# Rotary key projection of a diffusion backbone on one Trainium2 core: two products a chunk in place of three

## The reference

```python
D_MODEL, Q_LORA, KV_LORA, QK_ROPE, LRU_WIDTH, DEPTH = 1024, 384, 256, 32, 1024, 2
h = rms_norm(x, g_pre_mix) * (1.0 + sc1) + sh1
proj = h @ w_in            # columns: 384 query latent | 256 key/value latent | 32 rotary key | 1024 lru_x | 1024 lru_gate | 2048 merge
# query latent, kv latent: RMS norm, then up-projections to heads, attention
# rotary key (32 columns): axial rotation for the sample, shared by all 8 heads
# lru_x: centred convolution, two gates, a forward and a backward scan (RG-LRU)
# lru_gate: gelu;  merge: sigmoid gates of the two branches
```

## Time and profile before

| | |
|---|---|
| Median of 3 runs | 1290.33 us (1288.76 to 1290.85) |
| Profiled execution, device time | 1289.83 us |
| Its span, first to last instruction | 1288.0 us |
| PE busy | 1259.7 us (98%), 7748 matmuls |
| PEld busy | 1163.7 us (90%) |
| DVE busy | 803.5 us (62%), 1424 instructions |
| ACT busy | 660.5 us (51%), 1170 instructions |
| POOL busy | 18.4 us (1%) |
| DMA | 199.39 MB, mean 155 GB/s |
| Mean granted TensorE clock | 0.998 |
| Chain that ended last | PE 87%, DVE 5%, ACT 4%, issue 2%, DMA 2% |

### The profile page before, as it was taken

The page is one execution under the profiler, slowest core; times in us unless marked ns, Lnnn a source line. Parts: engine busy times, 40 slices in busy tenths (PEclk is TensorE's granted clock), DMA queues, the critical chain, the costliest instruction groups (busy, mean ns, idle before and its releaser), DMA issues.

```text
span 1288.0 us, 20162 instructions
## 1 busy us (share of the span) xinstructions
PE 1259.7 (98%) x7748; PEld 1163.7 (90%) x7748; DVE 803.5 (62%) x1424; ACT 660.5 (51%) x1170; POOL 18.4 (1%) x41
## 2 busy tenths in 40 slices
PE   6999999999999999999999999999999999999998
PEld 4999999978889999998889999998798899999886
DVE  2697584764858877743368786756566884433423
ACT  5379873754464333342266989457445533333422
POOL 0000000200000000000000000011000000000000
PEclk9999999999999999999999999999999999999999
DMA  9645555333346766545425546463225464444451
GB/s 335 202 121 175 191 153 195 105 115 120 119 128 205 228 212 212 164 139 176 123 63 166 156 132 203 130 227 112 102 77 162 149 200 131 132 131 131 156 164 49
DMA packets 138275, 199.39 MB, mean 155 GB/s; under 512 B 10330, under 2 KB 70980, under 8 KB 138180
## 3 DMA queue, kind: packets, MB, share of 16 engines
q1 hardware_dynamic: 138180, 198.11, 48.3%
HBM read 196.16 MB, written 1.92 MB: 154 GB/s over the span
## 4 chain that ended last, share of the span: by engine, by line
PE 87%; DVE 5%; ACT 4%; issue 2%; DMA 2%; SPq 0%; DVEq 0%; ACTq 0%
PE bank L698 19%; PE bank L705 18%; PE bank L706 18%; PE bank L801 5%; PE bank L803 5%; PE bank L802 5%; PE bank L735 2%; DVE weight_low L1607 1%; PE bank L1096 1%; PE bank L658 1%; ACT sq L1235 1%; PE bank L1120 1%; ACT weight_high L1227 1%; PE bank L1105 1%; PE bank L939 1%
## 5 line engine op out<-in xcount | busy, mean ns | idle before, releaser
L705 PE MATMUL bank<-act_low,weight_high 128*128 128x384 f32 x1440 | 486.8, 338 | 0.6 <-DVE weight_low L1607 0.6
L706 PE MATMUL bank<-act_high,weight_low 128*128 128x384 f32 x1440 | 482.6, 335 | 0.0
L1607 DVE TENSOR_TENSOR weight_low<-raw,weight_high 128x1024 fp32r<-128x1024 f32 (+5 forms) x282 | 320.1, 1152 | 211.4 <-ACT weight_high L1227 210.7
L1227 ACT ACTIVATE weight_high<-raw 128x1024 fp32r<-128x1024 f32 (+5 forms) x282 | 272.8, 995 | 227.8 <-PE bank L803 86.6
L698 PE MATMUL bank<-act_high,weight_high 128*128 128x384 f32 x1440 | 314.6, 338 | 1.8 <-DVE t L1704 1.8
L705 PEld LDWEIGHTS bank<-act_low,weight_high 128*128 128x128 f32 x1440 | 270.9, 188 | 6.7 <-issue 4.9
L706 PEld LDWEIGHTS bank<-act_high,weight_low 128*128 128x128 f32 x1440 | 270.9, 188 | 0.0
L698 PEld LDWEIGHTS bank<-act_high,weight_high 128*128 128x128 f32 x1440 | 252.6, 188 | 8.4 <-issue 5.3
L801 PE MATMUL bank<-weight_high,hid_high 128*128 128x512 f32 x264 | 103.0, 390 | 0.0
L803 PE MATMUL bank<-weight_high,hid_low 128*128 128x512 f32 x264 | 102.8, 389 | 0.0
L802 PE MATMUL bank<-weight_low,hid_high 128*128 128x512 f32 x264 | 102.8, 389 | 0.0
(11 more groups left out here) (249 smaller groups left out, 1512.7 us busy)
## 6 DMA issues: line engine op xcount, KB each, us to landing
raw<-in_w_ffn_in SPq DMA_DIRECT2D x176, 256.0 KB, 3.8
mod_weight<-in_w_mod SPq DMA_DIRECT2D x80, 512.0 KB, 4.8
raw<-in_w_in SPq DMA_DIRECT2D x72, 512.0 KB, 4.0
raw<-in_w_ffn_out SPq DMA_DIRECT2D x44, 512.0 KB, 3.8
first_mod<-in_w_mod SPq DMA_DIRECT2D x4, 2048.0 KB, 13.9
raw<-in_w_o_lru SPq DMA_DIRECT2D x16, 512.0 KB, 3.7
raw<-in_w_out SPq DMA_DIRECT2D x16, 512.0 KB, 3.7
raw<-in_w_o_mla SPq DMA_DIRECT2D x8, 512.0 KB, 4.7
```

Of the source, the lines that this page charges most:

```text
L705: nc.tensor.matmul(o, view[0][:, kk, cols], low[:, k, :], start=False, stop=False)
L706: ins = nc.tensor.matmul(o, view[1][:, kk, cols], high[:, k, :], start=False, stop=k == total - 1)
L1227: nc.scalar.activation(high, w, ACT.Copy).then_inc(*AC.step())
L1607: nc.vector.tensor_tensor(low, w, high.bitcast(F), ALU.subtract).then_inc(*VE.step())
```

## The change

The 160 columns of `kr` are laid out anew: the high part of all 160 stands in `weight_high` at a pitch of 224 columns, and behind each row's 160 stand the low parts of its last 64 columns. `weight_low` holds only the low parts of the first 128.

- TensorE: `rope_job` in place of `split_job`. The latent group takes three products a chunk as before. The second group is the columns 96 to 223 of the new layout: 64 high and 64 low columns. It takes two products a chunk, with the high and with the low activations. Output rows 32 to 63 then hold the rotary key by the high weights, rows 96 to 127 that by the low weights.
- ScalarE: one strided instruction a load makes the high part. For group 5 it copies 32 rows of the bank (rows 32 to 63) to the last 32 partitions of `qkv`, where it copied 128.
- VectorE: two subtractions a load in place of one. A new addition of 32x384 (step `rope`) adds rows 96 to 127 of the bank to what ScalarE left. It stands behind `squared_roots(2)` and waits for ScalarE's copy.
- The readers of `kr`'s banks are now given by the step `rope` of VectorE.

```diff
+KR, KR_LOW = 160, 64
+def rope_view(w, load):
+    return w[:, 0:load.kc * (KR + KR_LOW)].rearrange("p (k n) -> p k n", n=KR + KR_LOW)
@@ jobs
-        jobs += [("kr", [(AC, "qkv", 5)]), ("gg0", [(AC, "gate_input", 3)]), ("gg1", [(AC, "gelu", 7)])]
+        jobs += [("kr", [(VE, "rope")]), ("gg0", [(AC, "gate_input", 3)]), ("gg1", [(AC, "gelu", 7)])]
@@ TensorE
+                def rope_job(high, low):
+                    banks_free("kr")
+                    k = 0
+                    for n in of_job("kr"):
+                        load = LOADS[n]
+                        s = SIDX[n] % SPL
+                        pe.wait_ge(*at(AC, "high", n))
+                        whole = rope_view(wh[s], load)
+                        latent_low = wl[s][:, 0:load.kc * P].rearrange("p (k n) -> p k n", n=P)
+                        for kk in range(load.kc):
+                            latent, rope = bank("kr", 0)[:, 0:T], bank("kr", 1)[:, 0:T]
+                            nc.tensor.matmul(latent, whole[:, kk, 0:P], high[:, k, :], start=k == 0, stop=False)
+                            nc.tensor.matmul(latent, whole[:, kk, 0:P], low[:, k, :], start=False, stop=False)
+                            if kk == 0:
+                                pe.wait_ge(*at(VE, "low", n))
+                            ins = nc.tensor.matmul(latent, latent_low[:, kk, :], high[:, k, :], start=False, stop=k == C - 1)
+                            if k == C - 1:
+                                ins.then_inc(*PE.step("kr", 0))
+                            both = whole[:, kk, KR - KR_LOW:KR + KR_LOW]
+                            nc.tensor.matmul(rope, both, high[:, k, :], start=k == 0, stop=False)
+                            ins = nc.tensor.matmul(rope, both, low[:, k, :], start=False, stop=k == C - 1)
+                            if kk == load.kc - 1:
+                                ins.then_inc(*PE.step(*(("kr", 1) if k == C - 1 else ())))
+                                PE.also("used", n)
+                            k += 1
-                split_job("kr", hh, hl, groups=[slice(0, P), slice(160 - P, 160)])
+                rope_job(hh, hl)
@@ ScalarE, highs
-                        for high, w in pieces(LOADS[n], wh[m % SPL], raw[m % RAW]):
+                        if LOADS[n].job == "kr":
+                            w = raw[m % RAW][:, 0:LOADS[n].kc * KR].rearrange("p (k n) -> p k n", n=KR)
+                            high_pieces = [(rope_view(wh[m % SPL], LOADS[n])[:, :, 0:KR], w)]
...
@@ ScalarE, latents
+                    else:
+                        nc.scalar.activation(qkv[P - ROPE:P, c, :], bank(job, b)[KR_LOW - ROPE:KR_LOW, 0:T], ACT.Copy
+                                             ).then_inc(*AC.step("qkv", c))
@@ VectorE, lows
+                        if LOADS[n].job == "kr":
...
+                            low_pieces = [(latent_low, w[:, :, 0:P], whole[:, :, 0:P]),
+                                          (whole[:, :, KR:KR + KR_LOW], w[:, :, KR - KR_LOW:KR], whole[:, :, KR - KR_LOW:KR])]
...
@@ VectorE, list of the layer
                 squared_roots(2)
+                ve.wait_ge(*at(AC, "qkv", 5))
+                tail = slice(P - ROPE, P)
+                nc.vector.tensor_tensor(qkv[tail, 5, :], bank("kr", 1)[tail, 0:T], qkv[tail, 5, :], ALU.add).then_inc(*VE.step("rope"))
                 lows("gg0", 3)
```

More of the change, by code:

```diff
@@ L1225, in highs @@
                         ac.wait_ge(*atm(PE, "used", SPLIT[m - SPL], prev=m < SPL))
-                        for high, w in pieces(LOADS[n], wh[m % SPL], raw[m % RAW]):
+                        if LOADS[n].job == "kr":
+                            w = raw[m % RAW][:, 0:LOADS[n].kc * KR].rearrange("p (k n) -> p k n", n=KR)
+                            high_pieces = [(rope_view(wh[m % SPL], LOADS[n])[:, :, 0:KR], w)]
+                        else:
+                            high_pieces = pieces(LOADS[n], wh[m % SPL], raw[m % RAW])
+                        for high, w in high_pieces:
                             nc.scalar.activation(high, w, ACT.Copy).then_inc(*AC.step())
@@ L1425, in latents @@
                         nc.scalar.activation(latent_sq[c], bank(job, b)[:, 0:T], ACT.Square).then_inc(*AC.step("sqq", c))
-                    nc.scalar.activation(qkv[:, c, :], bank(job, b)[:, 0:T], ACT.Copy).then_inc(*AC.step("qkv", c))
+                    if c < 5:
+                        nc.scalar.activation(qkv[:, c, :], bank(job, b)[:, 0:T], ACT.Copy).then_inc(*AC.step("qkv", c))
+                    else:
+                        nc.scalar.activation(qkv[P - ROPE:P, c, :], bank(job, b)[KR_LOW - ROPE:KR_LOW, 0:T], ACT.Copy
+                                             ).then_inc(*AC.step("qkv", c))
                 lru_gates(0, (("gates0", 1), ("qk", 3), ("kr", 0), ("kr", 2)))
@@ L1604, in lows @@
                         ve.wait_ge(*in_layer(lm)(AC, "high", n))
-                        for (low, w), (high, _) in zip(pieces(LOADS[n], wl[m % SPL], raw[m % RAW]),
-                                                       pieces(LOADS[n], wh[m % SPL], raw[m % RAW])):
+                        if LOADS[n].job == "kr":
+                            kc = LOADS[n].kc
+                            w = raw[m % RAW][:, 0:kc * KR].rearrange("p (k n) -> p k n", n=KR)
+                            whole = rope_view(wh[m % SPL], LOADS[n])
+                            latent_low = wl[m % SPL][:, 0:kc * P].rearrange("p (k n) -> p k n", n=P)
+                            low_pieces = [(latent_low, w[:, :, 0:P], whole[:, :, 0:P]),
+                                          (whole[:, :, KR:KR + KR_LOW], w[:, :, KR - KR_LOW:KR], whole[:, :, KR - KR_LOW:KR])]
+                        else:
+                            low_pieces = [(low, w, high) for (low, w), (high, _) in zip(pieces(LOADS[n], wl[m % SPL], raw[m % RAW]),
+                                                                                        pieces(LOADS[n], wh[m % SPL], raw[m % RAW]))]
+                        for low, w, high in low_pieces:
                             nc.vector.tensor_tensor(low, w, high.bitcast(F), ALU.subtract).then_inc(*VE.step())
```

## The result

The changed kernel took 1293.46 us (median of 9 runs, 1291.24 to 1294.4) against 1289.49 for the kernel before (9 runs on the same chip, 1287.45 to 1290.86). The ratio is 1.0029, interval [1.0019, 1.0040]: slower by 0.29%, 3.7 us. The forecast was 1291.7 us, and its wider range ended at 1292.8. The sign came true; the time lies outside the range, and the loss is more than twice the +1.4 us of the sum. The profiled execution took 1292.93 us with a span of 1291.0, 3.0 more than before. One of the 11 executions of one later kernel (copy of group 5 first) took 3566.84 us and is left out of its ratio.

A forecast was written before the change was run, and what follows sets the result against it. VectorE and ScalarE, not 98%-busy PE, were taken to set gg1's start. Only the addition counted: 2 x 0.68 = +1.36 us on 1289.83 gives 1291.2, plus 0.50 for the median 1291.7 us; wider range 1289.7 to 1292.8.

The forecast's parts named there:

- The sign: Whole kernel: the change was forecast to be slower, 1291.7 us against a median of 1290.33.
- the +1.4 us of the sum: Whole kernel: the addition's 0.68 us at gg1 in each of two layers, together +1.36 us, all other terms nothing.
- PE's saving, nothing arrives: kr to gg1: eight matmuls fewer save 1.41 us a layer, but PE's resumption hangs on VectorE, so nothing arrives.
- ScalarE, nothing: ScalarE in kr: high parts have as many elements, group 5's copy costs the same on 32 partitions; no cost.
- Low parts split, hidden: VectorE's split low parts for kr: 0.48 us more a layer, covered by its 3.88 us wait for ScalarE.
- The addition, +0.68 us a layer, fully on the path: VectorE behind squared_roots(2): the new addition delays gg1's low part and PE's resumption by 0.68 us a layer.
- So no new wait arises and nothing is given back: Behind gg1's wait: PE sets the pace, VectorE and ScalarE shift by the same 0.68 us; no further cost or gain.
- the forecast's own range: Whole kernel: 1290.6 to 1292.4 us, given 73%; both bounds of the addition and 0.4 us for the median.
- The clock: Rival, 6%: longer waits at gg0's last and gg1's first load lower PE's clock; 5.0 us lost, 1295.3 us.
- the case of the 8%: Whole kernel slower by over 0.2%, above 1292.9 us: falling clock plus a small remainder for a VectorE cascade; chance 0.08.
- The saving arrives: Rival, 5%: in kr, each matmul less is time less, giving 1287.5 us, faster by over 0.2%.
- the addition is hidden: Rival, 16%: addition hidden or starting earlier, PE's gg1 resumption stays at 123.60; no effect, 1290.3 us (1289.5 to 1290.9).

The follow-up runs named there:

- copy of group 5 first: Changed kernel padded with 4 unread products, addition early, ScalarE copying group 5 after step 2 and group 4 after step 3: 1289.88 us, ratio 1.0002.
- the runs with the early addition: Changed kernel with group 5 copied right behind group 4 and the addition between squared_roots(1)'s halves: 1292.88 us; also with 4 unread products a layer: 1291.31 us.
- the repeat: The changed kernel measured again with no edit: 1292.73 us, ratio 1.0030 to the kernel before.
- padded: Changed kernel plus 4 unread float32 products (8 pairs) a layer at the end of kr, restoring TensorE's instruction count: 1291.45 us, ratio 1.0018.
- padded, no addition: Changed kernel without the addition and with 4 unread float32 products a layer at the end of kr: 1289.55 us, ratio 1.0004.
- code's place alone: Kernel before plus 56 float32 products (112 pairs) of two columns in PE's first wait: 1307.81 us, ratio 1.0137.
- addition alone: Kernel before plus one 32x384 VectorE operation (a maximum, changing no value) behind squared_roots(2): 1290.69 us, ratio 1.0011.

## Why the prediction was wrong

The terms up to `gg1` were right. The step that failed is the one from there to the end of the kernel, where the sum has nothing.

**PE's saving, nothing arrives: right.** `kr` takes 6.99 us (103.64 - 96.65), forecast 7.0. That is 1.45 us less, and PE waits 0.73 + 1.47 = 2.20 us a layer, forecast 2.2. The run without the addition shows the bare step: `gg1` at +0.01 and 0.00.

**ScalarE, nothing: the result is right in this place, the reason given is not.** The prediction has the copy on 32 partitions cost what the one on 128 did. From the start of the high part ahead of it to the start of the operation behind it, it is 1.59 us (108.71 to 110.30), where it was 1.32 (109.41 to 110.73): 0.27 us more a layer. That was covered, since ScalarE later waits for VectorE, 0.28 us in place of 0.54. In the runs with the early addition the same copy was on the chain and cost 0.64 us.

**Low parts split, hidden: right.** VectorE still waits for ScalarE behind them:

```profile
99.96 1.23 DVE L1662 TENSOR_TENSOR weight_low<-raw,weight_high 128x1024 fp32r<-128x1024 f32 x1 [3.41 <-ACT weight_high L1269]
```

It is 3.41 us in place of 3.88, less by 0.47; the estimate was 0.48.

**The addition, +0.68 us a layer, fully on the path: right.** Measured 0.72 a layer, alone and in the change. It starts 0.03 us behind the end of its forerunner (114.78 + 1.02 = 115.80), and the low part 0.04 behind its own end. The estimate took this from the operations at partition 64; by overlap it would have been 0.47.

**"So no new wait arises and nothing is given back": this step failed.** It took everything behind `gg1` as rigidly shifted by 0.68. A new wait does arise behind it, in `m2a` of layer 1, for a load that lands late. PE's part was costed as time only: eight pairs fewer at 0.176 us. That they are also 16 instructions fewer in TensorE's code a layer, 32 by the end of layer 1's `kr`, stood nowhere in the sum. The term left out is the packet of code at the issue of `m2a`'s loads: +2.07 us in the profiled execution, +1.01 in the repeat. In the medians: the change 1.0029 and 1.0030 against 1.0018 padded, about 0.0011 or 1.5 us; without the addition 1.0018 against 1.0004, 1.8 us. The addition is the rest, 1.0018 (padded) against 1.0004 (padded, no addition), 1.8 us where the traces give 1.44. (The kernel with neither ran on another chip than the rest of these.) Both together are 3.3 us and, with the 0.0004 of the kernel with neither, which isn't told from none, about the measured 3.7. The padded kernel, which has the addition but not the late load, took 1291.45 us, inside the forecast's own range.

Nothing in the trace of before would have given the size, but the place could have been named. The page of the profile counts 62 packets on q8, and the trace of before has one at 772.5, 1.5 us ahead of an issue for whose loads ScalarE already waits 1.76 us. A change of TensorE's code ahead of it moves the one against the other.

**The rivals.** The clock did not fall: granted 1.00 through and behind the waits of up to 1.47 us. The rows give a stretch, its length, the busy times of PE, PEld, DVE, ACT and POOL, and then the granted clock:

```profile
103.64:121.29 17.65, 16.92 (x98) 16.60 (x97) 13.81 (x27) 17.05 (x26) 0.00 (x0) 1.00 0.53 164
...
747.52:775.00 27.48, 26.02 (x172) 25.00 (x172) 22.82 (x43) 23.46 (x39) 0.00 (x0) 1.00 0.45 134
775.00:820.00 45.00, 43.38 (x316) 40.06 (x316) 31.24 (x64) 36.36 (x56) 0.00 (x0) 1.00 0.57 178
```

So the case of the 8%, slower by over 0.2%, came true, by a cause that none of the rivals named. "The saving arrives" and "the addition is hidden" are refuted by `gg1`'s +0.72.

**What stays open.** In all 13 profiles the length of SyncE's issue goes with the packet's place. In five it runs in the first 0.5 us of the issue, and the issue takes 1.59 to 1.97 us (the change, its repeat, without addition, addition early, code's place alone). In eight it runs 0.8 to 1.5 us ahead, and the issue takes 0.88 or 0.89 (before, addition alone, and all that are padded). The same goes on elsewhere, but not each time: over the 13 traces, 66 of the 141 issues of one weight load that start between 0.1 us ahead of such a packet and 0.5 behind it take over 0.6 us, and 98 of the 5008 that have none within 2 us; the usual one takes 0.37. And it need not cost anything: at 760.06 the changed kernel has another such pair of `mod_weight` issues, 1.59 us for 0.91, and PE's offset is 1.8 on both sides of it. Why the packet holds up the issue no row shows, nor where the 1.06 us behind the issue come from; and moving the loads instead of the code was not tried. That q8 carries TensorE's code is inferred from the count of 256 and from its packets moving with the padding.

## What to carry to other kernels

Work taken from an engine that waits at the end of the same stretch only lengthens its wait; look for the engine that sets the end, and put what it waits for earlier (the low part ahead of the roots: 0.94 us a layer between the kernels with and without it, in which the matmuls were already fewer). An added operation in a gapless chain costs its full step, and its input may stand on the same chain: moving it into a wait of VectorE only moved the cost to ScalarE's copy, until that copy took the place of something longer. If two versions differ by a microsecond or two at places that the edit does not touch, compare them matmul by matmul and with TensorE's instruction count padded to equal, before the edit gets the credit or the blame.

## What the runs showed of the hardware

- In five traces a 16 KB packet of q8 (kind "instruction") falls on SyncE's issue of two 512 KB loads ahead of `m2a`. The issue then takes 1.59 to 1.97 us in place of 0.88, and the load behind it, in the changed kernel, feeds ScalarE 2.1 us later. The Trainium skill (page "Runtime: NRT & Kernel Launch", section "Instruction fetch mechanics") says that an engine's code is refilled in blocks of 16 KiB, 256 instructions, at a cost that is mostly hidden. The trace agrees on the block (1.02 MB in 62 packets) and the count (15,875 instructions). The cost is hidden from TensorE at that moment, which has no idle time at 776 us, but not from SyncE's loads.
- ScalarE's copy of 32 partitions (from rows 32 to 63 to the last 32) between operations on 128 starts 0.51 us behind the copy ahead, after its end, and the next one starts 0.50 or 0.51 us behind it, again after its end. In the kernel before, the operation behind a copy of 128 partitions starts 0.37 us behind it.
- 56 float32 products of two columns in TensorE's first wait moved everything behind them by 16.3 us. What of it is their own time and what the start of the kernel, I did not take apart.
